# Transposes of the output stage split over two PSUM banks, in a hybrid attention layer on eight cores

## What is computed

```
u = rms_norm(h) @ w_in                     # 1024 -> 5376: q, k, v, z of two mixers, two merge gates
qa, ka, qb, kb = per-head rms_norm of each
oa = window attention (2 chunks before + own, ALiBi, sinks);  ob = band attention (8 chunks before + own)
branch_a = (oa * silu(za)) @ w_o_win       # 512 -> 1024
branch_b = (ob * silu(zb)) @ w_o_band      # 512 -> 1024
h = h + (sigmoid(ga) * branch_a + sigmoid(gb) * branch_b) @ w_out
h = h + sigmoid(rms_norm(h) @ w_ple_gate) * (p @ w_ple)
```

## Time and profile before

| what | us |
|---|---|
| median of 2 runs | 1658.68 (1657.25 to 1660.11) |
| the profiled execution, its time | 1658.72 |
| its span on the slowest core (core 3) | 1657.2 |
| spans of all eight cores | 1646.8 to 1657.2 |
| granted TensorE clock, mean by core | 0.966 to 0.973 |

### The profile page before, as it was taken

How to read it: one execution, slowest core, us unless ns; L and a number is a source line. 1 busy time by engine, 2 the same in 40 slices (tenths; PEclk the granted TensorE clock), 3 DMA queues, 4 the chain that set the end, 5 groups by cost and what they waited for, 6 DMA issues and landing times.

```text
span 1657.2 us, 26270 instructions; the slowest of 8 cores (1646.8 to 1657.2 us)
## 1 busy us (share of the span) xinstructions
PE 1406.0 (85%) x9636; PEld 693.7 (42%) x9636; DVE 845.5 (51%) x1711; ACT 792.5 (48%) x1396; POOL 385.7 (23%) x488
## 2 busy tenths in 40 slices
PE   0688888898999888988899899888988888988864
PEld 0344344444444444444444444444444444444431
DVE  1344455555555555555555555555555554454632
ACT  1353455555555454555555555545455545444341
POOL 4221122222222222222222222222212222222310
PEclk9899999999999999999999999999999999989877
DMA  9998434544444445444444444344444445336452
GB/s 183 189 162 138 119 112 125 131 130 117 114 113 114 118 131 131 114 112 117 130 131 121 115 118 111 112 130 131 122 113 113 124 131 136 105 110 160 98 136 70
DMA packets 107681, 206.51 MB, mean 125 GB/s; under 512 B 16672, under 2 KB 23840, under 8 KB 107392
## 3 DMA queue, kind: packets, MB, share of 16 engines
q1 hardware_dynamic: 94272, 185.33, 41.3%
q0 software_dynamic: 13280, 19.50, 8.7%
HBM read 204.69 MB, written 25.69 MB: 139 GB/s over the span
## 4 chain that ended last, share of the span: by engine, by line
PE 50%; DVE 22%; POOL 8%; ACT 6%; DMA 5%; another core or an unknown queue 4%; issue 4%; POOLq 0%; ACTq 0%; SPq 0%; DVEq 0%
PE psmm L121 26%; PE pstl L121 15%; POOL st L111 7%; DVE st L111 5%; PE pss L121 5%; DVE xb L111 5%; DVE pstl L111 4%; DVE qkn L111 4%; DVE pss L111 3%; PE pso L121 3%; DMA W_in<-w_in 2%; ACT t1t L111 2%; ACT ET L111 2%; DMA wring<-wsc 2%
## 5 line engine op out<-in xcount | busy, mean ns | idle before, releaser
L121 PE MATMUL psmm<-W_in,xnT 128*128 128x512 bf16 (+1 forms) x3000 | 692.5, 376 | 69.3 <-DVE qkn L111 39.8
L121 PEld LDWEIGHTS psmm<-W_in,xnT 128*128 128x128 bf16 x3000 | 284.8, 100 | 396.6 <-DVE qkn L111 50.3
L111 ACT ACTIVATE ET<-pss 128x512 bf16<-128x512 f32 x440 | 256.2, 597 | 198.9 <-DVE pss L111 123.7
L121 PE MATMUL pstl<-wring,actT 128*128 128x512 bf16 x1056 | 316.0, 389 | 14.0 <-DMA wring<-wsc 9.0
L111 POOL TENSOR_TENSOR st<-st,mhalf 128x8 f32<-128x8 f32 (+2 forms) x177 | 216.1, 1221 | 475.5 <-DVE st L111 341.6
L111 POOL TENSOR_TENSOR ybuf<-ont,zs 128x256 bf16<-128x256 f32 x132 | 88.5, 670 | 303.5 <-DVE ont L111 299.1
L111 ACT ACTIVATE sqt<-psmm 128x512 f32<-128x512 f32 (+1 forms) x140 | 71.9, 514 | 178.6 <-PE psmm L121 173.2
L111 ACT ACTIVATE tg<-psmm 128x512 bf16<-128x512 f32 x132 | 78.6, 595 | 155.0 <-PE psmm L121 155.0
L111 DVE TENSOR_TENSOR pss<-pss,tabBs 128x512 f32<-128x512 f32 x132 | 86.5, 693 | 101.7 <-PE pss L121 101.7
L111 DVE TENSOR_TENSOR pss<-pss,tabAs 128x512 f32<-128x512 f32 x132 | 91.4, 694 | 72.0 <-PE pss L111 72.0
L121 PE MATMUL pss<-qbT,kbT 64*128 64x128 bf16 x1320 | 125.9, 220 | 2.0 <-ACT ET L111 0.8
(11 more groups left out here) (87 smaller groups left out, 1428.7 us busy)
## 6 DMA issues: line engine op xcount, KB each, us to landing
wring<-wsc SPq DMA_DIRECT2D x528, 256.0 KB, 3.9
xb<-xm SPq DMA_DIRECT2D x32, 512.0 KB, 4.5
y<-xb SPq DMA_DIRECT2D x32, 512.0 KB, 2.8
W_in<-w_in POOLq DMA_DIRECT2D x2, 2560.0 KB, 86.8
W_in<-w_in POOLq DMA_DIRECT2D x2, 2048.0 KB, 51.2
pb<-pm SPq DMA_DIRECT2D x32, 128.0 KB, 3.3
xb<-xh SPq DMA_DIRECT2D x4, 512.0 KB, 20.3
wsc<-w_out POOLq DMA_DIRECT2D x1, 2048.0 KB, 124.9
```

Of the source, the lines that this page charges most:

```text
L111: inst = getattr(e, method)(*args, **kw)
L121: last = getattr(e, m)(*a, **k)
```

## The change

`transposes8` writes transposes 0 to 3 into pstl0 and 4 to 7 into pstl1, as two groups of four, each with its own dependency. After the first two uses ACT copies half 0 out of pstl0 and DVE half 1 out of pstl1. After the third use the one DVE multiply over 1024 columns becomes two over 512, one for each bank. Everything else, the planner included, is as it was; the planner gets the new operations and makes its order again.

```diff
-        def transposes8(src, sres_):
-            S.group("pe", [("transpose", (trz[:, c * 128:(c + 1) * 128], src[:, c * 128:(c + 1) * 128], ident[:]), {})
-                           for c in range(8)], r=[sres_, "ident"], w=[TL[0]])
+        trzs = [ps_tl[0][:].bitcast(BF16), ps_tl[1][:].bitcast(BF16)]
+
+        def transposes8(src, sres_, banks=None):
+            if banks is None:
+                banks = [(trzs[0], TL[0]), (trzs[1], TL[1])]
+            for hf in range(2):
+                tb, tres_ = banks[hf]
+                S.group("pe", [("transpose", (tb[:, c * 128:(c + 1) * 128],
+                                              src[:, (4 * hf + c) * 128:(4 * hf + c + 1) * 128], ident[:]), {})
+                               for c in range(4)], r=[sres_, "ident"], w=[tres_])
+            return banks
+
+        def evac_plain(banks):
+            S.ins("act", "copy", actT[:, 0:512], banks[0][0][:, 0:512], r=[banks[0][1]], w=["actT_a"])
+            S.ins("dve", "tensor_copy", out=actT[:, 512:1024], in_=banks[1][0][:, 0:512], r=[banks[1][1]], w=["actT_b"])
...
-        transposes8(ybuf, yres)
-        S.ins("act", "copy", actT[:, 0:512], trz[:, 0:512], r=[TL[0]], w=["actT_a"])
-        S.ins("dve", "tensor_copy", out=actT[:, 512:1024], in_=trz[:, 512:1024], r=[TL[0]], w=["actT_b"])
+        evac_plain(transposes8(ybuf, yres))
...
-        transposes8(mbuf, "mbuf")
-        S.ins("act", "copy", actT[:, 0:512], trz[:, 0:512], r=[TL[0]], w=["actT_a"])
-        S.ins("dve", "tensor_copy", out=actT[:, 512:1024], in_=trz[:, 512:1024], r=[TL[0]], w=["actT_b"])
+        evac_plain(transposes8(mbuf, "mbuf"))
...
-        transposes8(mbuf, "mbuf")
-        S.ins("dve", "tensor_tensor", out=v3(actT[:], 128), in0=v3(trz[:, :], 128), in1=bc3(gTple[:, 0:8], 128),
-              op=ALU.mult, r=[TL[0], "gTple"], w=["actT_a", "actT_b"])
+        bk = transposes8(mbuf, "mbuf")
+        for hf in range(2):
+            S.ins("dve", "tensor_tensor", out=v3(actT[:, hf * 512:(hf + 1) * 512], 128), in0=v3(bk[hf][0][:, 0:512], 128),
+                  in1=bc3(gTple[:, 4 * hf:4 * hf + 4], 128), op=ALU.mult, r=[bk[hf][1], "gTple"],
+                  w=["actT_a" if hf == 0 else "actT_b"])
```

## The result

The changed kernel takes 1670.2 us (median of 11 runs) against 1659.5 for the kernel before (10 runs) on the same chip: ratio 1.0072 [1.0061, 1.0083], 0.72% slower where I had forecast 1.3% faster. The profiled execution has a span of 1667.1 us on its slowest core (core 3 again), 9.9 more than before, and a granted clock of 0.964 to 0.968 by core.

A forecast was written before the change was run, and what follows sets the result against it. PE was taken as full except 4.33 us idle a tile, mostly latency at the tile boundary. Gain 1.16 - 0.50 = 0.66 us a tile, times 30 is 19.8, plus 1.5: 1658.7 - 21.3 = 1637 us, range 1605 to 1680.

The forecast's parts named there:

- PE's clock as unchanged: PE's busy time, by its clock or the longer distance between its groups, was taken as unchanged; no price given.
- Part 1: First transposes and W_ow product: ACT's copy and W_ow begin about 0.2 us earlier a tile; serial copies already cost nothing.
- Part 2: DVE behind W_ow: t1 half 0 goes ahead of the ka norm's multiply, norm chain 0.95 us later, net loss 0.50 a tile.
- The tie of 0.02: On DVE, planner costs make t1 half 0 ready at 2.57, the ka norm's multiply at 2.59, putting t1 ahead by 0.02 us.
- -0.50: Net loss a tile from the delayed norm chain, 0.95 us late, less about 0.45 as the second transposes fill PE's wait.
- Part 3: Stage Z ends over 1 us earlier, so attention's last work fills PE's waits for t1 and pT: gain 1.16 us a tile.
- the 1.16: PE's waits at stage Z's end, 0.69 for t1 plus 0.47 for pT a tile, all expected to be filled.
- Part 4: DVE's two multiplies after the third transposes: 0.155 us more, 33 times, covered by 1.5 us: cost 0, at most 5.1 us.
- Part 5: Last tile, no other work beside it: W_ob starts 1.2 us earlier; with parallel copies 1.5 us gained at the end.
- absorbed: Rival: what one wait of PE wins returns at the next; only the last tile gains, 1657 us; chance 0.20.
- Slower: Rival: both t1 halves pass norm steps on DVE, 1.55 us late, 1.35 net a tile, 39 us, 1698 us; chance 0.18.

The follow-up runs named there:

- oldorder_newbanks: The changed kernel's instructions (two banks, parallel copies, two multiplies), issued in the order planned for the kernel before: 1656.31 us beside 1656.64, ratio 0.9995.
- the tie run: The changed kernel with 0.03 us more planner cost per W_ow group, so DVE runs the ka norm's multiply ahead of t1 half 0: 1662.3 us, ratio 1.0033 to before.
- neworder_oldbanks: The kernel before (one bank, serial copies, one multiply), issued in the order planned for the changed kernel: 1695.9 us, ratio 1.0238 to before.
- the doubled scores: The changed kernel, order untouched, with 12 of mixer B's score matmuls per tile computed twice into the same place: 1654.6 us, ratio 0.9988 to before.

## Why the prediction was wrong, step by step

- **The assumption that decided: PE's clock as unchanged.** The text named it as one that would make it wrong ("if PE's busy time itself changes, by its clock … which I take as unchanged"), and gave it neither a price nor a chance. It costs 1.68 us where it happens, in 11 periods and with 2.8 more in the first about 20 us on the profiled core; without it the changed kernel runs at 1654.6 even with extra work. What I should have asked: the earlier trace rows show PE waiting 0.75 for an exponential, and the earlier trace rows a clock of 1.00; a change that moves fillers out of attention makes exactly such stretches lighter. The Trainium skill (TensorE: Matmul & The Clock Gate, "A second HAM failure mode: psum-queue depth-cycling") says of another kernel that frequent micro-idle gaps between matmul groups make the clock oscillate between its two levels. The trace agrees: gaps of 0.38 and 0.58 us ahead of a 1.90 us group that takes 3.37.
- **Part 1, W_ow: the direction right, the size near.** "They run at about 816.75" was right in kind: half 1's transposes do wait for DVE's xb, 0.33 us a tile. The wait of 0.77 is gone, 0.4 net instead of 0.2. The copies do not overlap, as its times had them, and the serial copies were no cost in the old order, which oldorder_newbanks shows (1656.3 against 1656.6). That nothing is to be counted between a DVE copy and POOL's power held as well: the power at 831.15 takes 0.70 beside the copy at 831.17.
- **Part 2, the order: right; its price: wrong.** The tie of 0.02 fell as computed, and the multiply was 0.92 late (0.95 forecast). But a late step is not a late chain: the multiply of kb's norm starts only 0.17 later, the wait for qkn, which was to rise above 50.1 us, fell to 43.6, and the tie run has the better place for the multiply and the longer period (45.66). As an order it was worth about +0.5 a tile, not -0.50.
- **Part 3, the failed size: "the last scores and values of attention lie beside it and fill these waits".** Stage Z came earlier and t1's wait fell from 0.69 to 0.19, but pT's stayed (0.47, now 0.46), 0.5 of the 1.16. The step took attention as a filler that costs nothing. It is itself in need of one: before, w_out pairs and projection groups stood between its scores and values, and with Z ahead some of them were already done, so PE waited for exponentials instead: 55.8 us in all, from 24.1. The idle time in an undisturbed period is only 4.33 - 3.78 = 0.55 less, and the period is 0.16 longer, where 0.7 shorter was forecast (44.3), as PE's busy time rose by 0.71 at full clock. That busy time rises with the same 287 matmuls fits what the Trainium skill says (Trainium Kernel Development and Optimization, its note on reading a trace): since matmuls are pipelined, it is a bad measure of how near a kernel is to its limit. The number of separate groups rose and the number of matmuls did not, which may be the reason; no run shows it.
- **Part 4, DVE's extra instructions cost nothing: right.** DVE's busy time is 845.1 against 845.5, and the third split alone has no loss. That it wins 12.5 us was outside my range for it (a cost of 0 to 5.1 us).
- **Part 5, the last tile: right in kind.** There the copies do overlap, in the changed kernel:

```profile
1629.53 0.59 ACT L111 COPY actT<-pstl 128x512 bf16<-128x512 bf16 x1 [2.79 <-PE pstl L121]
1629.96 0.42 DVE L111 COPY actT<-pstl 128x512 bf16<-128x512 bf16 x1 [1.94 <-PE pstl L121]
...
1651.27 1.29 DVE L111 TENSOR_TENSOR actT<-pstl,gTples 128x512 bf16<-128x512 bf16 x2 [2.67 <-PE pstl L121]
```

The last seven tiles and the decoding tile gain 14.1 us together on this core, and 6 to 15 by core, far more than the 1.5 for the end. Neither the split nor the new order does it alone: this stretch takes 341.2 to 346.1 us by core in oldorder_newbanks and 340.1 to 345.2 in neworder_oldbanks, but 332.5 to 334.6 with both.
- **The rivals.** Without the falls the kernel would lie near 1650 by the account (1670 less some 20), and with the doubled scores it lies at 1654.6: between my 1637 and the 1657 of "absorbed", and nearer to that. "Slower" had the sign and not the mechanism: the norm chain came 0.17 later, not 1.35, and its price of 39 us is not what was paid. The range of 1605 to 1680 held the time.

## What to carry to other kernels

When a planner inside the kernel makes the order, a local change is two changes: run the new instructions in the old order (here 0.9995) before you credit or blame the mechanism, and correct the planner's costs before you judge it (here a loss of 12 us became a gain of 40). Before either figure is put down to the change, count the falls of the clock in both kernels: they were the loss, and by the estimate above over half of the gain. When PE's busy time grows with the same number of matmuls, look at the granted clock by window: a few stretches in which PE does only small matmuls and waits for another engine can cost more than the waits themselves. Matmuls of no use in such a gap can then be worth their time, and they are also the experiment that shows whether the clock is the cause.

## What the hardware showed that I had not expected

- A fall of the clock does not need a long pause: PE was busy for 1.99 of 2.95 us with scores and values, its longest wait was 0.58, and the clock was 0.50 from 812.0 to 815.4. It does not follow each time, either: the same stretch, with 2.00 of 2.95, left the clock at 1.00 one period later. What in such a stretch counts, the waits, or the kind of matmul (64 rows of the array, or 65 columns), no run tells apart.
- More work made a kernel faster twice: 12 doubled matmuls a tile won 13.9 us, and six idle ones 30 us, where the same doubling without falls to prevent cost 0.0068 x 1656.8 = 11 us.
- Two DVE multiplies of 512 columns back to back, in the last tile, take 1.29 us against 1.22 for one of 1024, half of the extra 0.155 that I had counted.
